# Stick-breaking attention: a running product over keys on VectorE instead of triangular matmuls

## What is computed

```python
def stick_breaking_attention(q, k, v):
    ...
        z = jnp.einsum('bqhd,bkhd->bhqk', q_blk, k, preferred_element_type=jnp.float32) * scale
        earlier = key_pos[None, :] < q_pos[:, None]
        log_keep = jnp.where(earlier, jax.nn.log_sigmoid(-z), 0.0)
        log_after = lax.cumsum(log_keep, axis=3, reverse=True) - log_keep
        weight = jnp.where(earlier, jnp.exp(jax.nn.log_sigmoid(z) + log_after), 0.0)
        return jnp.einsum('bhqk,bkhd->bqhd', weight.astype(v.dtype), v)
```

## Time and profile before

| | us |
|---|---|
| median of three runs | 2203.21 (2202.31 to 2203.70) |
| the profiled run's own time | 2203.45 |
| its span | 2201.7 |
| PE busy | 2179.6 (99%) |
| DVE busy | 1221.3 (55%) |
| ACT busy | 928.3 (42%) |
| POOL busy | 171.1 (8%) |

### The profile page before, as it was taken

The page is one execution under the profiler, slowest core; times in us unless marked ns, Lnnn a source line. Parts: engine busy times, 40 slices in busy tenths (PEclk is TensorE's granted clock), DMA queues, the critical chain, the costliest instruction groups (busy, mean ns, idle before and its releaser), DMA issues.

```text
span 2201.7 us, 26347 instructions
## 1 busy us (share of the span) xinstructions
PE 2179.6 (99%) x10252; PEld 1704.3 (77%) x10252; DVE 1221.3 (55%) x1859; ACT 928.3 (42%) x1519; POOL 171.1 (8%) x276
## 2 busy tenths in 40 slices
PE   9999999999999999999999999999999999999999
PEld 7768778678888888886666788888886667888887
DVE  5674874565544444554345655554647586555454
ACT  4464444554433222424445433333345665333331
POOL 0000422111000000102222000000011000000000
PEclk9999999999999999999999999999999999999999
DMA  5212112123323232321111222332322112233233
GB/s 179 78 50 95 49 42 91 40 84 110 102 96 96 97 98 93 105 87 59 48 48 47 88 96 96 105 96 88 104 86 68 58 49 77 96 105 96 93 99 106
DMA packets 52108, 187.05 MB, mean 85 GB/s; under 512 B 5904, under 2 KB 6032, under 8 KB 51856
## 3 DMA queue, kind: packets, MB, share of 16 engines
q1 hardware_dynamic: 51840, 185.18, 25.9%
q10 hardware_dynamic: 144, 0.18, 0.0%
HBM read 183.25 MB, written 2.10 MB: 84 GB/s over the span
## 4 chain that ended last, share of the span: by engine, by line
PE 93%; DVE 4%; ACT 2%; issue 1%; DMA 0%; SPq 0%; DVEq 0%; ACTq 0%
PE ps L1011 23%; PE ps L1014 23%; PE ps L1017 22%; PE ps L1035 4%; PE ps L1038 4%; PE ps L1036 4%; PE ps L990 2%; PE ps L1350 2%; PE ps L1088 1%; PE ps L1140 1%; PE ps L1338 1%; PE ps L1325 1%; PE ps L1355 1%; PE ps L1112 1%; PE ps L1158 1%
## 5 line engine op out<-in xcount | busy, mean ns | idle before, releaser
L1404 ACT CAST wh<-raw 128x1024 fp32r<-128x1024 f32 x334 | 350.2, 1048 | 872.2 <-PE ps L1017 792.7
L1751 DVE TENSOR_TENSOR wl<-raw,wh 128x1024 fp32r<-128x1024 f32 (+2 forms) x338 | 413.9, 1225 | 173.2 <-ACT wh L1404 172.5
L1011 PE MATMUL ps<-hh,wh 128*128 128x512 f32 x1408 | 449.7, 400 | 4.1 <-DVE F L1900 2.8
L1014 PE MATMUL ps<-hh,wl 128*128 128x512 f32 x1408 | 435.5, 390 | 2.4 <-DVE wl L1751 2.4
L1017 PE MATMUL ps<-hl,wh 128*128 128x512 f32 x1408 | 434.8, 390 | 0.0
L1014 PEld LDWEIGHTS ps<-hh,wl 128*128 128x128 f32 x1408 | 264.4, 188 | 59.5 <-DVE wl L1751 3.6
L1017 PEld LDWEIGHTS ps<-hl,wh 128*128 128x128 f32 x1408 | 264.6, 188 | 56.5 <-DVE hl L1832 0.2
L1011 PEld LDWEIGHTS ps<-hh,wh 128*128 128x128 f32 x1408 | 258.6, 188 | 62.4 <-issue 9.7
L1011 PE MATMUL ps<-R,wh 128*128 128x512 f32 x896 | 287.1, 401 | 0.0
L1014 PE MATMUL ps<-R,wl 128*128 128x512 f32 x896 | 277.4, 390 | 0.5 <-DVE wl L1751 0.5
L1017 PE MATMUL ps<-R,wh 128*128 128x512 f32 x896 | 276.9, 390 | 0.0
(11 more groups left out here) (230 smaller groups left out, 2121.1 us busy)
## 6 DMA issues: line engine op xcount, KB each, us to landing
raw<-in_weights SPq DMA_DIRECT2D x332, 512.0 KB, 3.3
x<-in_x_t SPq DMA_DIRECT2D x4, 512.0 KB, 7.0
F<-in_x_t SPq DMA_DIRECT2D x4, 512.0 KB, 4.4
out<-x SPq DMA_DIRECT2D x8, 256.0 KB, 2.0
raw<-in_weights SPq DMA_DIRECT2D x4, 416.0 KB, 3.1
x<-in_bias SPq DMA_DIRECT2D x1, 1024.0 KB, 7.5
F<-in_weights SPq DMA_DIRECT2D x2, 384.0 KB, 3.8
F<-in_weights SPq DMA_DIRECT2D x2, 256.0 KB, 5.1
```

Of the source, the lines that this page charges most:

```text
L1011: pe.matmul(out, hi[:, k, cs], B.tile(u.src, k)[0], start=k == 0, stop=False)
L1014: pe.matmul(out, lo[:, k, cs], B.tile(u.src, k)[0], start=False, stop=False)
L1404: act.copy(B.wh[s][:, 0:nk * ncol], B.raw[s][:, 0:nk * ncol]).then_inc(S["w_hi"], 1)
L1751: dve.tensor_tensor(lo, src, hi.bitcast(F32), ALU.subtract).then_inc(S[name], 1)
```

## The change

Queries now lie on the partitions. An item is a pair of heads with one or two blocks of 128 queries against all keys up to that block: query block 3 (4 blocks of 128 x 128 for each head, 512 columns), 2 (3 blocks, 384 columns), or 0 and 1 (1 + 2 blocks, 384 columns). Step s of a group does:

- TensorE: eight or six transposes of the weights of item s - 2 (`sb_turn`), the product of item s - 3 in blocks of 128 columns (`sb_product`), the scores of item s (`sb_scores`). The products with `negU` and with minus ones are gone.
- ACT: one copy of the turned weights of item s - 2 out of two banks, then two sigmoids over two banks each for item s, of z (`beta`) and of -z (`keep`). Another table of functions is loaded at the first step and the old one at the end.
- DVE: for item s - 1 one `tensor_tensor_scan` for each head, backward along the keys, in place: the running product of `keep`, with a maximum against a row of zeros and ones (`sb_floor`) that sets it to 1 at and behind the diagonal; then one multiply of `beta` by the product shifted by one key.
- GpSimd: one mask of `beta`'s diagonal blocks for each item, and once the array of zeros and ones.

The scores of a group use one pair of banks (4 and 5 in group 0, 6 and 7 in group 1), the transposes the other, the outputs 0 and 1, and `uv[1]` rotates over 2, 3, 0, 5, which gives its four parts the banks 0, 5, 2, 3. The dense steps and their order are as before. Lines of the new kernel: 995 transposes, 1339 products, 1357 scores, 2224 scans, 2227 multiply, 1711 copy, 1724 and 1726 sigmoids; the dense matmuls are 1016, 1019, 1022 and 1040, 1041, 1043, `split` is 1416, `split_low` 1768.

```diff
-SB_X, SB_O = ((4, 5), (0, 6)), (1, 7)
+SB_X, SB_T, SB_O = (4, 6), (6, 4), (0, 1)
...
         self.run(self.dense(uv[0]))
+        self.add("sb_mask")
         self.banks = (2, 3)
...
-        self.banks = (0, 1, 2, 3)
+        self.banks = (2, 3, 0, 5)
         self.run(self.dense(uv[1], {1: first[13], 4: first[14], 14: second[0]}))
...
-    return 12 * g + s, s // 3, ((2, 3), (1,), (0,))[s % 3]
...
+    return 12 * g + s, s // 3, ((3,), (2,), (0, 1))[s % 3]
...
+    def sb_turn(g, s):
+        v, _, qts = sb_item(g, s)
+        w = B.sb_beta(v)
+        two = [empty(SB_T[g] + hf) for hf in range(2)]
+        at.wait_ge("sb_w", v + 1)
+        for hf in range(2):
+            last = transposes(two[hf], [w[:, hf, j * P:(j + 1) * P] for j in range(len(sb_blocks(qts)))])
+        last.then_inc(S["sb_t"], 1)
+        for hf in range(2):
+            emptied[SB_T[g] + hf] = (("sb_p", v + 1),)
+    def sb_product(g, s):
+        v, p, qts = sb_item(g, s)
+        b, turned, v4 = SB_O[p % 2], B.sb_turned(v), B.f4("F8" if g else "F3")
+        if s % 3 == 0:
+            empty(b)
+        at.wait_ge("sb_p", v + 1)
+        for kt in range(4):
+            at.wait_ge(*plan.freed(plan.uv[g][0], kt)[0])
+        for j, (qt, kt) in enumerate(sb_blocks(qts)):
+            for hf in range(2):
+                h = 2 * p + hf
+                last = pe.matmul(B.bank[b][64 * hf:64 * hf + 64, qt * P:(qt + 1) * P], v4[:, kt, h * 64:(h + 1) * 64],
+                                 turned[:, hf, j * P:(j + 1) * P], start=s % 3 == 0 and j == 0, stop=kt == qt,
+                                 skip_group_check=True)
+        last.then_inc(S["sb_o"], 1)
+        if s % 3 == 2:
+            emptied[b] = (("sb_yh", 4 * g + p + 1), ("sb_yl", 4 * g + p + 1))
+    def sb_scores(g, s):
+        q, k = (B.f4(f) for f in (("F4", "F6") if g else ("F0", "F2")))
+        v, p, qts = sb_item(g, s)
+        two = [empty(SB_X[g] + hf) for hf in range(2)]
+        for name, value in plan.freed(plan.uq[g][p], 0) + plan.freed(plan.uk[g][p], 0):
+            at.wait_ge(name, value)
+        o = 0
+        for qt in qts:
+            n = (qt + 1) * P
+            for hf in range(2):
+                rr = slice(64 * hf, 64 * hf + 64)
+                last = pe.matmul(two[hf][:, o:o + n], q[rr, p, qt * P:(qt + 1) * P], k[rr, p, 0:n], start=True, stop=True)
+            o += n
+        last.then_inc(S["sb_z"], 1)
+        for hf in range(2):
+            emptied[SB_X[g] + hf] = (("sb_g", v + 1),)
     def sb(g, s):
-        q, k, v4 = (B.f4(f) for f in (("F4", "F6", "F8") if g else ("F0", "F2", "F3")))
+        if 2 <= s < 14:
+            sb_turn(g, s - 2)
         if 3 <= s:
-            v, p, kts = sb_item(g, s - 3)
...
+            sb_product(g, s - 3)
         if s < 12:
-            v, p, kts = sb_item(g, s)
...
+            sb_scores(g, s)
     def dt(u, h):
...
     def sb(g, s):
-        for hf in range(2):
...
+        if g == 0 and s == 0:
+            load_table(SIGMOID)
+        if 2 <= s < 14:
+            v, _, qts = sb_item(g, s - 2)
+            n = sb_width(qts)
+            at.wait_ge("sb_t", v + 1)
+            at.wait_ge("sb_o", v - 1)
+            act.copy(B.sb_turned(v)[:, :, 0:n], B.two_banks(SB_T[g])[:, :, 0:n]).then_inc(S["sb_p"], 1)
+        if 3 <= s and s % 3 == 2:
+            v, p, _ = sb_item(g, s - 3)
+            at.wait_ge("sb_o", v + 1)
+            act.copy(B.R[2 * g][:, p * T:(p + 1) * T], B.bank[SB_O[p % 2]][:]).then_inc(S["sb_yh"], 1)
+        if s < 12:
+            v, _, qts = sb_item(g, s)
+            n = sb_width(qts)
+            z = B.two_banks(SB_X[g])[:, :, 0:n]
+            if v < 2:
+                at.wait_ge("fin_x", 8)
+            at.wait_ge("sb_z", v + 1)
+            at.wait_ge("sb_t", v - 1)
+            act.activation(B.sb_beta(v)[:, :, 0:n], z, ACT.Sigmoid).then_inc(S["sb_b"], 1)
+            at.wait_ge("sb_w", v - 1)
+            act.activation(B.sb_keep(v)[:, :, 0:n], z, ACT.Sigmoid, scale=-1.0).then_inc(S["sb_g"], 1)
+        if g == 1 and s == 12:
+            load_table()
...
     def sb(g, s):
-        if s < 12:
...
+        if 1 <= s < 13:
+            v, _, qts = sb_item(g, s - 1)
+            n = sb_width(qts)
+            keep, weight = B.sb_keep(v), B.sb_beta(v)
+            at.wait_ge("sb_f", 2)
+            at.wait_ge("sb_g", v + 1)
             for hf in range(2):
-                dve.tensor_scalar(B.sb_weights(v, hf)[:, 0:n], B.bank[SB_X[v % 2][hf]][:, 0:n], 30.0, None,
...
+                back = keep[:, hf, n - 1::-1]
+                dve.tensor_tensor_scan(back, back, B.sb_floor(qts)[:, ::-1], 1.0, ALU.mult, ALU.max).then_inc(S["sb_c"], 1)
+            at.wait_ge("sb_m", v + 1)
+            at.wait_ge("sb_c", 2 * v + 2)
+            dve.tensor_tensor(weight[:, :, 0:n - 1], weight[:, :, 0:n - 1], keep[:, :, 1:n], ALU.mult).then_inc(S["sb_w"], 1)
+        if 3 <= s and s % 3 == 2:
+            _, p, _ = sb_item(g, s - 3)
+            ys = slice(p * T, (p + 1) * T)
+            at.wait_ge("sb_yh", 4 * g + p + 1)
+            low(B.R[2 * g + 1][:, ys], B.bank[SB_O[p % 2]][:], B.R[2 * g][:, ys], "sb_yl")
...
-    def earlier(ap, kts, name):
-
+    def sb_mask():
+        floor = B.sb_mask()
+        at.wait_ge("n_st", 3)
         alone()
-        pattern = [[1, P]] if len(kts) == 1 else [[0, len(kts)], [1, P]]
...
+        pool.memset(floor, 0.0).then_inc(S["sb_f"], 1)
+        ran("sb_f")
+        alone()
+        ends = floor[:, 2 * P:6 * P].rearrange("p (b k) -> p b k", b=2)[:, :, P:2 * P]
+        pool.affine_select(out=ends, in_=ends, compare_op=ALU.is_gt, fill=1.0, base=0, pattern=[[0, 2], [-1, P]],
+                           channel_multiplier=1).then_inc(S["sb_f"], 1)
+        ran("sb_f")
     def sb(g, s):
-        if 1 <= s < 13 and sb_item(g, s - 1)[2][0]:
...
+        if s < 12:
+            v, _, qts = sb_item(g, s)
+            ap, pattern = sb_diagonals(B.sb_beta(v), qts)
+            at.wait_ge("sb_b", v + 1)
+            alone()
+            pool.affine_select(out=ap, in_=ap, compare_op=ALU.is_gt, fill=0.0, base=0, pattern=pattern,
+                               channel_multiplier=1).then_inc(S["sb_m"], 1)
+            ran("sb_m")
```

More of the change, by code:

```diff
@@ L20 @@
 EPS = 1e-6
+LOG_EXP, SIGMOID = 6, 2
 LAM_INIT = 0.8 - 0.6 * float(np.exp(-0.3))
@@ L847, in h_keys, with sb_beta, sb_keep, sb_turned @@
         return self.W[4 + n % 4]
[L849 to L861, removed]
+    def sb_beta(self, v):
+        o = 1024 * (v % 2)
+        return self.F["F7"][:, o:o + 1024].rearrange("p (h k) -> p h k", h=2)
+    def sb_keep(self, v):
+        o = 1024 * (v % 2)
+        return self.F["F1"][:, o:o + 1024].rearrange("p (h k) -> p h k", h=2)
+    def sb_turned(self, v):
+        o = 1024 * (v % 2)
+        return self.F["F5"][:, o:o + 1024].rearrange("p (h k) -> p h k", h=2)
+    def sb_mask(self):
+        return self.C[:, NCONST:NCONST + SCRATCH]
+    def sb_floor(self, qts):
+        o, n = {3: 0, 2: P, 0: 3 * P}[qts[0]], sb_width(qts)
+        return self.sb_mask()[:, o:o + n]
     def k_state(self):
@@ L910, in sb_item, with sb_blocks, sb_width, sb_diagonals @@
 def sb_item(g, s):
-    return 12 * g + s, s // 3, ((2, 3), (1,), (0,))[s % 3]
[L915 to L933, removed]
+    return 12 * g + s, s // 3, ((3,), (2,), (0, 1))[s % 3]
+def sb_blocks(qts):
+    return [(qt, kt) for qt in qts for kt in range(qt + 1)]
+def sb_width(qts):
+    return P * len(sb_blocks(qts))
+def sb_diagonals(ap, qts):
+    if len(qts) == 1:
+        return ap[:, :, qts[0] * P:qts[0] * P + P], [[0, 2], [-1, P]]
+    return ap.rearrange("p h (b k) -> p h b k", b=2)[:, :, :, 0:P], [[0, 2], [0, 2], [-1, P]]
 def h_pair(p, lv):
@@ L1343, in sb @@
-        if 1 <= s < 13:
-            v, p, kts = sb_item(g, s - 1)
-            for hf in range(2):
-                bank = B.bank[SB_X[v % 2][hf]]
-                at.wait_ge("sb_l", 2 * v + hf + 1)
-                at.wait_ge("sb_p", 2 * v + hf + 1)
-                n = sb_width(kts)
-                last = pe.matmul(bank[:, 0:n], B.const("negU"), B.sb_item_logs(kts, hf), start=False, stop=True,
-                                 skip_group_check=True)
-                if kts[0] < 2:
-                    at.wait_ge("sb_sp", sb_adds(v - 1))
-                kt, _, e = sb_spans(kts)[0]
-                last = pe.matmul(bank[:, P:e], B.const("negones"), B.sb_logs(kt + 1, hf), start=False, stop=True,
-                                 skip_group_check=True)
-                last.then_inc(S["sb_u"], 1)
+            sb_product(g, s - 3)
```

81 lines of the change are left out of this document (4 added, 77 removed).

## The result

| | before | after | change |
|---|---|---|---|
| median, us | 2203.41 (2202.31 to 2203.70) | 2164.21 (2164.18 to 2164.25) | -39.2, ratio 0.982 (0.981 to 0.983) |
| span of the profiled run | 2201.7 | 2162.5 | -39.2 |
| attention stage | 1006 to 1200 | 1006 to 1161 | |

The account below looks back on a forecast made before the run. TensorE was taken as the bound, busy 99% of the span; -55.0 - 2.1 + 19.6 + 0 - 4.25 + 3.7 = -38.05 from the profiled run's 2203.45 gave 2165 us, range 2157 to 2176.

Parts of the forecast that it names:

- triangular products with their slow restarts: On TensorE, products with `negU` and minus ones go, with slow dense restarts: 6.88 us a head pair, eight pairs, -55.0 us.
- starts behind dense matmuls: On TensorE, 24 steps now begin with transposes, which start without the extra 0.08 to 0.09 us: -2.1 us.
- transposes: New on TensorE: 20 a pair in three steps, 0.109 us each plus 0.09 a change, eight pairs: +19.6 us.
- products with the values: On TensorE, same columns cut in 128-column blocks, three blocks 0.77 us against 0.80 today: 0.
- scores: On TensorE, same widths, with queries in the place of keys: 0.
- stall behind `uv[1]` and clock: TensorE's 3.0 us stall after `uv[1]` and 1.7 of lower clock go, a 0.45 wait is left: -4.25 us.
- waits for weights: TensorE's transposes wait for DVE's multiply at items 0, 9, 12 and 21: 1.0, 0.3, 1.4, 1.0, together +3.7 us.
- 4 us kept for short blocks: In the range only: short product blocks might hide weight loads worse, perhaps 0.05 us a block, 80 blocks, +4 us.
- Rival (5): The triangular products cost nothing because PE waited there anyway; this or nothing gained, near 2200 us, chance 0.02.
- rival (1): Scans on DVE take one pass, leaving no wait but 0.3 us: 2162 us, chance 0.14.
- Rival (4): Each of the four waits lowers TensorE's clock, a fall costing 1.7 us: 2172 us, chance 0.07.
- Rivals (2) and (3): (2) DVE leads, 2184 us at 4.2 ns an element, chance 0.08; (3) scan waits out each write, 2231, 0.03.

Follow-up runs that it names:

- tri_gone: The kernel before without any product with `negU` or minus ones, what waited for them waiting for GpSimd's mask; ACT, DVE and GpSimd keep their work: 2175.45 us.
- one_pass: The changed kernel with each scan replaced by one elementwise maximum on the same reversed, in-place operands: 2161.93 us.
- uvrot: The changed kernel with only the banks of `uv[1]` changed, to 2, 0, 5, 3 for its four parts: 2164.33 us.
- load2: The changed kernel with two more DVE passes over each item's `keep`, result unchanged, 4.9 ns for each scanned element: 2200.16 us.

## Why the prediction was right, step by step

The distances between starts on PE, added up over the stage by kind, before and after:

| | predicted | measured |
|---|---|---|
| triangular products with their slow restarts | -55.0 | -53.2 without the restarts |
| starts behind dense matmuls | -2.1 | -3.9 with those restarts; the remainder of the whole |
| transposes | +19.6 | +19.8 |
| products with the values | 0 | 20.8 to 21.1: +0.3 |
| scores | 0 | 22.2 to 22.1: -0.1 |
| stall behind `uv[1]` and clock | -4.25 | -2.6 and -1.7: -4.3 |
| waits for weights | +3.7 | +2.2 |
| sum | -38.05 | -39.2 |

**What went, what came.** The first two rows together are -57.1 as predicted and -57.1 as measured. The second is a remainder, but the dense matmuls give it too: their distances sum to 98.0 us before and 92.2 after, with one more of 0.23 in the window; less stall, clock and waits that is -3.9. So every term on TensorE itself was right to 0.3 us, since all were read as distances between starts and not as lengths. The 4 us kept for short blocks weren't needed: three blocks take 0.80, where 0.77 was said and 0.80 stood before.

**The -55.0 had a condition that the prediction didn't state.** `tri_gone` shows that the same 55 us taken out of the old kernel give 28. In the prediction the term went through because the new chain was then followed item by item. What it didn't say is that the old chain (clip, Exp, Ln, maximum, mask, Exp) lived in the cover of these very products, and that about half of the 55 us depends on ACT losing Exp and Ln. That the scores' banks are free after the second sigmoid should help as well; no run shows it alone. Rival (5), at 2200, comes nearest, but it has PE waiting already beside the old products, and the kernel before shows no such wait.

**The scan.** Two passes were taken, 1.22 and 0.96; 1.21 and 0.95 came. With rival (1)'s price `one_pass` ran in 2161.93, where 2162 was said.

**The waits.** This is the term that was mis-sized, 3.7 against 2.2: 1.0 was 0.80 at item 0, 0.3 was nothing at item 9, 1.4 was 0.65 at item 12, 1.0 was 0.72 at item 21. The places were right, three of four. The chain at item 12 shows where the rest lies:

```profile
1092.62 1.02 ACT L1724 ACTIVATE F<-ps 128x1024 f32<-128x1024 f32 x1 [4.09 <-PE ps L1357]
...
1093.54 1.02 ACT L1726 ACTIVATE F<-ps 128x1024 f32<-128x1024 f32 x1
...
1094.44 1.27 ACT L1474 ACTIVATE F<-ps,st 128x512 f32<-128x512 f32 x2
...
1095.58 1.07 ACT L1416 CAST wh<-raw 128x1024 fp32r<-128x1024 f32 x1
...
1096.75 1.23 DVE L1768 TENSOR_TENSOR wl<-raw,wh 128x1024 fp32r<-128x1024 f32 x1 [2.50 <-ACT wh L1416]
...
1097.89 2.33 DVE L2224 TENSOR_TENSOR_SCAN F<-F,C 128x512 f32<-128x512 f32 x2
...
1101.70 1.06 PE L995 MATMUL ps<-C,F 128*128 128x128 f32 x8 [0.49 <-DVE F L2227]
```

A sigmoid is 1.02 long, but the next starts 0.92 after it; the two evacuations take 1.14 up to the cast, not 1.4. From the end of the scores, 1092.50, to the transposes at 1101.70 it was 9.2 where the lengths added up to 9.8, and the cover 8.55 where 8.4 was said. Of the 0.6 between them 0.36 lies at the sigmoids and 0.26 at the evacuations; cast and `split_low` together were right to 0.05, and the scans with their multiply took the 3.8 that was said (1097.89 to 1101.70). Items 0 and 21 took 7.5 from the end of the scores to the transposes where 7.7 was said, 0.1 of it at the evacuation ahead of the scans (0.60 and 0.61 to the scan's start, not 0.69). So the prediction read TensorE by starts and the operations ahead of the scans by lengths, and the second was the error, about 0.1 for each operation behind another.

**The stall and the clock.** Both as predicted, with a wait of 0.41 left where 0.45 was said, but `uvrot` shows that this wait cost nothing: item 12's would have been that much longer. The assumption "nothing shorter than that 3 us gap lowered it" was safe for the three waits here (0.9 to 1.0 between starts), and too high as a bound: 2.30 was enough once. The 1.7 us for a fall was 1.5 by the times of single executions. Rival (4) didn't come, and 160 transposes in the stage at a granted clock of 1.00 speak against any danger from them. (The stretch 370 to 390 that the prediction called full of them holds 33, about 3.6 of its 20 us; this stage has 17.4 in 155.) The Trainium skill ("TensorE: Matmul & The Clock Gate", Part 4, PE-mode transpose) says that they do not count as work for the clock; no row here shows a fall that this would explain.

**Rivals (2) and (3).** At 3.3 ns an element the gain was to begin to melt, at 5.4 to be eaten. `load2` stood at 4.9 ns with 3.5 us of gain left, so 5.4 was somewhat high: another 3.5 / 20.0 = 0.18 ns gives 5.1.

## What to carry to other kernels

Before a piece of work is taken off the leading engine, ask what other engines do beneath it: here removing it alone gave half, and the other half came when ACT's Exp and Ln went too. Read every engine by distances between starts, also those off the path, if their chains are to be weighed against a cover of a few us. And look at the order in queues where the leading engine waits: moving one step gave the old kernel 4.1 us, moving three scans and the banks gave the new one 2.8, with no operation made cheaper, while the banks alone gave nothing because the next wait took it.

## What the runs showed of the hardware

- A float32 matmul of 16 columns on a full 128 x 128 stationary side is recorded 0.112 behind the one before, as one of 128 columns (0.109; 256 columns 0.216): narrower than 128 saved nothing.
- A scan over 512 columns takes 1209 ns and over 384 948, an elementwise operation with the same operands 686 and 581.
- The lower clock came in stretches of 3.4 us, once of 6.8, behind gaps of 2.3 us and more on TensorE, not behind every gap below 3.0, and behind one of 3.2 not in every execution. A fall cost 1.5 to 1.7 us, whatever the gap.
